# Sums added into the score bank of stick-breaking attention, and the attention layers' low weight halves on VectorE instead of GpSimd

## The chip, the cores and the metric

The kernel is one program on one core of a Trainium2 chip. Its engines are TensorE (PE; PEld is its weight load), VectorE (DVE), ScalarE (ACT), GpSimd (POOL) and SyncE (SP), which issues transfers. The metric is the device time of one execution in microseconds; lower is better.

## What is computed

The reference runs four mixer blocks on a sequence of 512 tokens of width 1024 (pooling, gated convolution, latent attention, pooling again), and behind them two layers that matter here. Each of these computes

```
h    = rmsnorm(x, attn_norm[l])
proj = h @ w_in[l]                      # sb_q, sb_k, sb_v, df_q, df_k, df_v
sb   = stick_breaking_attention(sb_q, sb_k, sb_v)       # 8 heads of 64
df   = differential_attention(df_q, df_k, df_v, lam)    # 4 heads
x    = x + concat(sb, rmsnorm(df) * c) @ w_o[l]
x    = x + square(relu(rmsnorm(x) @ w_ff1[l])) @ w_ff2[l]
```

For a head of the stick-breaking attention, with z the scaled scores of a query against all keys,

```
log_beta = log_sigmoid(z)
log_keep = where(key < query, log_sigmoid(-z), 0)
between  = reversed_cumsum(log_keep) - log_keep          # sum over later keys
w        = where(key < query, exp(log_beta + between), 0)
out      = w @ v
```

With s = softplus(z) = max(z, 0) + log(1 + exp(-|z|)), log_keep is -s and log_beta is z - s, and also min(z, 0) - log(1 + exp(-|z|)).

## The kernel before, in words

Each product of single precision is made of three matmuls on two-part operands: high times high, low times high, high times low (`mm3`, lines 489 to 492; `mm3_on`, lines 494 to 497). A tile of weights ("unit") of 128 rows and up to 1024 columns is loaded into one of four `raw` buffers; ScalarE writes its high part to one of three `wh` buffers (line 1283), and the low part, raw minus high, is written to one of three `wl` buffers by VectorE (line 2109) or by GpSimd in pieces of 256 columns (line 3170). TensorE then waits for `("wlo", n)` and uses the tile in 24 matmuls of 512 columns.

`unit_table` (line 139) lists the units in the order of their use. Its `low(True)` and `low(False)` mark from which unit on the low parts are GpSimd's; a mark takes effect `LOOK` = 2 units later. In each of the two last layers `low(True)` stands ahead of all 32 attention units and `low(False)` ahead of the last, ("wo", 1, 3).

Nothing is scheduled at run time. Each engine has a program of its own, written out by hand as a list of steps, and waits on semaphores for results of the others. In `second_layer(l)` of each engine the list says where it deals with a weight unit (`taking(...)` makes the high or low parts up to two units ahead), a projection (`project`, `turned`, `plain`, `rot`), a head of the stick-breaking attention and a head of the differential attention (`df_...`). VectorE's program had no `taking` in the attention part of these layers, as GpSimd had it.

One head h of the stick-breaking attention goes as follows. Its scores are triangular and are held as three groups of key blocks, (2, 3), (1) and (0), with 384, 384 and 512 columns, each in one of three PSUM banks kept for this purpose (`GR`, `sb_banks`).

- TensorE, `sb_scores(h)` and `sb_cover(h)`: z into bank "ss", with a large negative number added where key >= query.
- ScalarE, `soft(h)`: |z| from the bank (line 1741), exp (line 1745), log (line 1751), into the buffer SA.
- VectorE, `soft(h)`: min(z, 0) - SA into SL (line 2743), then max(z, 0) + SA into SA (line 2746), after which the bank is free.
- ScalarE and VectorE, `keep(h)`: high and low part of SA, SBH and SBL (lines 1292 and 2117).
- TensorE, `sb_between(h)`: sums over later keys, with a triangular matrix of ones `trir` (lines 985 and 986) and a full one `onesr` (lines 990 and 991), into bank "sb", which is the same bank as "ss" in its next use.
- VectorE, `between(h)`: SL minus the sums, into SA (line 2757); the bank is free after it.
- ScalarE, `weights_of(h)`: exp of SA (line 1764) and high part; VectorE: low part.
- TensorE, `sb_pv(h)`: times v (lines 1003 and 1004).

TensorE's order around the steps that are spoken of below, as written in its list:

```
sb_between(3)  df_pv(1)  df_scores(2, 32)  sb_scores(4)  df_scores(2, 16)  sb_cover(4)  proj("dk", 3) ...
df_squares(1)  sb_between(4)  df_turn(2)  proj("sk", 3)  df_pv(2)  df_scores(3, 34)  sb_scores(5) ...
sb_pv(4)  wo(0, 2)  wo(0, 0)  df_scores(3, 16)  sb_between(5)  wo(0, 1)  df_squares(2)  sb_scores(6) ...
sb_between(7)  wo(1, 0, ..)  wo(1, 1, ..)  wo(1, 4, ..)  sb_pv(7)
```

ScalarE's list has `df_turn(1)`, `df_exp(2, 34)`, `df_copy(1)`, `weights_of(3)`; later `df_exp(3, 16)`, `weights_of(5)`. The exponentials of `df_exp` (line 1534) wait for VectorE's `df_max` (lines 2461, 2465, 2468).

Of the kernel before, what the change touches and what calls it, by code (L numbers as in the profile page):

```python
# [138 lines left out]
def unit_table(D):  # L139
# [71 lines left out]
    for l in range(2):  # L211
        qk, v, wo = D[f"qk{l}"], D[f"v{l}"], D[f"wo{l}"]

        low(True)
        for kind, *key in LAYER_UNITS:
            if kind == "v":
                add(("v", l, *key), v[tuple(key)], 1024)
            elif kind == "wo":
                if key == [1, 3]:
                    low(False)  # L220
                add(("wo", l, *key), wo[tuple(key)], 1024)
            else:
                add((kind, l, *key), qk[0, {"sq": 0, "sk": 4, "dq": 8, "dk": 12}[kind] + key[0]], 1024)
# [90 lines left out]
def program(nc, D, out):  # L314
    ctx = ExitStack()
    with ctx:
# [60 lines left out]
        m_before, m_after = OB[:, 0:128], OB[:, 128:256]  # L377
# [29 lines left out]
        SA, SL, SBH, SBL = SETS[0]  # L407
# [59 lines left out]
        def pe_program(handle, c):  # L467
# [399 lines left out]
            def second_layer(l):  # L867
# [112 lines left out]
                def sb_between(h):  # L980
                    for n, (kbs, k0, width) in enumerate(GR):
                        for jb in range(kbs[0], 4):
                            pe.wait_ge(*at("kpl", l, h, {0: 0, 1: 1, 2: 2, 3: 2}[jb]))
                        b = use(sb_banks[n], ("sb", l, h, kbs[0]))
                        pe.do.matmul(b[:, 0:width], trir[:, :], SBH[:, k0:k0 + width], start=True, stop=False)
                        pe.do.matmul(b[:, 0:width], trir[:, :], SBL[:, k0:k0 + width], start=False, stop=False)
                        for jb in range(kbs[0] + 1, 4):
                            o = b[:, 128 * (jb - kbs[0]):512 - 128 * kbs[0]]
                            cc = slice(KOFF[jb], KOFF[jb] + 512 - 128 * jb)
                            pe.do.matmul(o, onesr[:, :], SBH[:, cc], start=False, stop=False)  # L990
                            mm = pe.do.matmul(o, onesr[:, :], SBL[:, cc], start=False, stop=jb == 3)
# [268 lines left out]
        def act_program(handle, c):  # L1260
# [420 lines left out]
            def second_layer(l):  # L1681
# [402 lines left out]
        def dve_program(handle, c):  # L2084
# [92 lines left out]
            def load():  # L2177
# [21 lines left out]
                dve.do.tensor_copy(trir[:, :], m_after)  # L2199
# [458 lines left out]
            def second_layer(l):  # L2658
# [79 lines left out]
                def soft(h):  # L2738
                    for kbs, k0, n in GR:
# [99 lines left out]
                if l == 0:  # L2839
                    scalars()  # L2840
                norms()
                both_norms()
                turn_by_norm()
                v_low(0, 0)
                if l:
                    scalars()
                project("sq", 0)
                plain("sq", 0)
                project("sk", 0)
                plain("sk", 0)  # L2850
                soft(0)
                keep(0)
                turned("dq", 0)
                v_low(0, 1)
                rot("dq", 0)
                between(0)
                turned("dk", 0)
                weights_of(0)
                rot("dk", 0)
# [807 lines left out]
```

## Time and profile before

| | |
|---|---|
| median of 3 runs | 2635.23 us (2634.94 to 2635.53) |
| the profiled execution | 2635.47 us |
| its span, first to last instruction | 2633.7 us |
| granted TensorE clock, mean | 1.000 |
| busy PE / PEld | 2621.3 / 2224.4 us |
| busy DVE / ACT / POOL | 1790.2 / 1310.9 / 608.1 us |

The span is the time from the first to the last instruction of the profiled execution; the execution's own time is 1.8 us longer. Busy times are unions of the instructions' durations. Those of matmuls overlap, because the engine is pipelined and their ends are modelled; the distance of two starts tells more than a duration. The two attention parts lie at about 1457 to 1714 us and 2052 to 2305 us of the span.

### The profile page before, as it was taken

To read this page: it belongs to the slowest core of one execution; us is meant where nothing else is said; L and a number is where in the kernel's file an instruction comes from. 1 tells how busy PE (TensorE), PEld (TensorE's weight loads), DVE (VectorE), ACT (ScalarE), POOL (GpSimd) and SP (SyncE) were. 2 spreads that over 40 slices of the span, in tenths; PEclk is the share of its full clock that TensorE was granted. 3 is DMA by queue.
4 is the path that set the end of the run, shared out by engine and by line. 5 is a ranking of instruction groups with operands and counts; after the bars stand their busy time and mean duration, and the time that the engine had idled before them with its cause. 6 is when DMAs were issued, how large, how long until landed. Compare 5 with 4: busy or idle time off the path is not lost.

```text
span 2633.7 us, 33670 instructions
## 1 busy us (share of the span) xinstructions
PE 2621.3 (100%) x13168; PEld 2224.4 (84%) x13168; DVE 1790.2 (68%) x2771; ACT 1310.9 (50%) x2086; POOL 608.1 (23%) x674
## 2 busy tenths in 40 slices
PE   9999999999999999999999999999999999999999
PEld 7888889899888888888888888888888888888887
DVE  7656576666666646666475768876777568876677
ACT  5323353334346636533225677754445677754445
POOL 0000111011026627510002744420100544420100
PEclk9999999999999999999999999999999999999999
DMA  4233266466322232232222421355651321355650
GB/s 168 96 97 99 89 167 157 132 157 160 111 66 65 69 89 60 73 103 96 96 96 74 124 85 49 110 149 154 176 152 43 106 71 49 122 151 148 176 144 32
DMA packets 92111, 287.13 MB, mean 109 GB/s; under 512 B 10928, under 2 KB 13488, under 8 KB 91952
## 3 DMA queue, kind: packets, MB, share of 16 engines
q1 hardware_dynamic: 80784, 257.18, 30.2%
q0 software_dynamic: 11168, 27.79, 6.4%
q8 instruction: 104, 1.70, 0.3%
q14 instruction: 55, 0.45, 0.1%
HBM read 274.45 MB, written 2.10 MB: 105 GB/s over the span
## 4 chain that ended last, share of the span: by engine, by line
PE 92%; DVE 5%; ACT 2%; issue 0%; POOL 0%; DMA 0%; SPq 0%; DVEq 0%; ACTq 0%
PE ps L490 26%; PE ps L491 26%; PE ps L492 26%; PE ps L497 3%; PE ps L496 3%; PE ps L495 3%; DVE ptl L2117 1%; PE ps L715 1%; PE ps L569 0%; DVE s L2746 0%; DVE s L2743 0%; PE ps L776 0%; PE ps L775 0%; ACT s L1534 0%; ACT s L1745 0%
## 5 line engine op out<-in xcount | busy, mean ns | idle before, releaser
L490 PE MATMUL ps<-xh,wh 128*128 128x512 f32 (+1 forms) x1808 | 696.7, 385 | 0.5 <-POOL wl L3170 0.5
L491 PE MATMUL ps<-xl,wh 128*128 128x512 f32 (+1 forms) x1808 | 692.6, 383 | 0.0
L492 PE MATMUL ps<-xh,wl 128*128 128x512 f32 (+1 forms) x1808 | 692.4, 383 | 0.0
L1283 ACT ACTIVATE wh<-raw 128x1024 fp32r<-128x1024 f32 (+3 forms) x387 | 389.7, 1008 | 481.1 <-PE ps L492 410.7
L2109 DVE TENSOR_TENSOR wl<-raw,wh 128x1024 fp32r<-128x1024 f32 (+2 forms) x277 | 331.2, 1196 | 110.8 <-ACT wh L1283 110.3
L490 PEld LDWEIGHTS ps<-xh,wh 128*128 128x128 f32 x1808 | 340.1, 188 | 67.6 <-POOL wl L3170 1.4
L492 PEld LDWEIGHTS ps<-xh,wl 128*128 128x128 f32 x1808 | 339.9, 188 | 66.6
L491 PEld LDWEIGHTS ps<-xl,wh 128*128 128x128 f32 x1808 | 340.1, 188 | 65.0 <-issue 1.0
L3170 POOL TENSOR_TENSOR wl<-raw,wh 128x256 fp32r<-128x256 f32 x392 | 302.5, 805 | 388.5 <-ACT wh L1283 362.1
L490 PE MATMUL ps<-yh,wh 128*128 128x512 f32 x640 | 251.4, 393 | 0.7 <-ACT s L1534 0.7
L491 PE MATMUL ps<-yl,wh 128*128 128x512 f32 x640 | 249.4, 390 | 0.0
L492 PE MATMUL ps<-yh,wl 128*128 128x512 f32 x640 | 249.4, 390 | 0.0
L3179 POOL TENSOR_TENSOR acc<-acc,t 128x512 f32<-128x512 f32 x44 | 61.7, 1402 | 717.6 <-ACT t L1304 716.3
L1283 ACT ACTIVATE wh<-a 128x1024 fp32r<-128x1024 f32 x96 | 101.9, 1062 | 126.8 <-PE ps L492 64.5
L490 PEld LDWEIGHTS ps<-yh,wh 128*128 128x128 f32 x640 | 120.2, 188 | 27.0 <-POOL wl L3170 2.0
L492 PEld LDWEIGHTS ps<-yh,wl 128*128 128x128 f32 x640 | 120.2, 188 | 25.3
L491 PEld LDWEIGHTS ps<-yl,wh 128*128 128x128 f32 x640 | 120.3, 188 | 23.9
L2109 DVE TENSOR_TENSOR wl<-a,wh 128x1024 fp32r<-128x1024 f32 x96 | 117.1, 1220 | 32.2 <-ACT wh L1283 32.1
L2146 DVE TENSOR_TENSOR x<-ps,x 128x512 f32<-128x512 f32 x96 | 65.4, 687 | 105.6 <-PE ps L492 105.5
L1292 ACT ACTIVATE yh<-t 128x512 fp32r<-128x512 f32 (+1 forms) x148 | 86.1, 584 | 100.4 <-DVE t L2250 56.3
L2117 DVE TENSOR_TENSOR yl<-t,yh 128x512 fp32r<-128x512 f32 (+1 forms) x148 | 99.8, 675 | 36.6 <-ACT yh L1292 36.6
L3103 DVE SCALAR_TENSOR_TENSOR t<-ps,r 128x512 f32<-128x512 f32 x64 | 44.1, 690 | 89.1 <-PE ps L492 88.8
(370 smaller groups left out, 5224.9 us busy)
## 6 DMA issues: line engine op xcount, KB each, us to landing
raw<-in_ff SPq DMA_DIRECT2D x64, 512.0 KB, 5.9
a<-in_ff2t SPq DMA_DIRECT2D x64, 512.0 KB, 7.5
raw<-in_pool_in SPq DMA_DIRECT2D x62, 512.0 KB, 3.4
raw<-in_conv_in SPq DMA_DIRECT2D x50, 512.0 KB, 4.0
raw<-in_pool_out SPq DMA_DIRECT2D x32, 512.0 KB, 3.4
raw<-in_qk SPq DMA_DIRECT2D x32, 512.0 KB, 3.6
sw<-in_conv_in SPq DMA_DIRECT2D x42, 256.0 KB, 3.9
raw<-in_pool_grp SPq DMA_DIRECT2D x16, 512.0 KB, 3.5
```

The source lines that it names most:

```text
L490: pe.do.matmul(o, lh, rh_, start=start, stop=False)
L491: pe.do.matmul(o, lh, rl_, start=False, stop=False)
L492: return pe.do.matmul(o, ll, rh_, start=False, stop=stop)
L495: pe.do.matmul(o, lh, rh_, start=False, stop=False, skip_group_check=True)
L496: pe.do.matmul(o, lh, rl_, start=False, stop=False, skip_group_check=True)
L497: return pe.do.matmul(o, ll, rh_, start=False, stop=stop, skip_group_check=True)
L1283: act.do.activation(h[:, 0:ncol], r[:, 0:ncol], ACT.Copy).then_inc(*mark("whi", ("whi", k)))
L1292: act.do.activation(dst, src, ACT.Copy).then_inc(*mark("act", done))
L2109: dve.do.tensor_tensor(lo[:, 0:ncol], r[:, 0:ncol], f(h[:, 0:ncol]), ALU.subtract).then_inc(*mark("wlo", ("wlo", k)))
L2117: dve.do.tensor_tensor(dst, src, f(h), ALU.subtract).then_inc(*mark("dve", *done))
L2146: dve.do.tensor_tensor(x[m][:, :], ps(*key)[:, :], x[m][:, :], ALU.add).then_inc(*mark("dve", ("psfree",) + key, *done))
L3170: p = pool.do.tensor_tensor(lo[:, cc], r[:, cc], f(h[:, cc]), ALU.subtract)
```

## The change

It does two things in the two last layers.

The sums are added on top of the scores. `sb_between(h)` writes into the bank that still holds z ("ss"), as further matmuls of the same accumulation. The kept values are split with a factor of -1 (ScalarE's copy has scale -1, VectorE's low part is `low_scaled` with -1), so that -s is added, and the triangular matrix is p >= n instead of p > n, so that the sum takes in the key itself: z - s - (sums over later keys). With that SL, line 2743 and the step `between(h)` on VectorE go. ScalarE's `weights_of(h)` takes the exponential from the bank, all three groups first and then the three high parts, and the bank is free after the exponential.

`low(True)` moves from the head of the layer to ("wo", 1, 1). VectorE's list gets a `taking(...)` at each place where the attention units are dealt with.

```
-        low(True)
         for kind, *key in LAYER_UNITS:
...
             elif kind == "wo":
+                if key == [1, 1]:
+                    low(True)
                 if key == [1, 3]:
                     low(False)
...
                 def sb_between(h):
...
-                        b = use(sb_banks[n], ("sb", l, h, kbs[0]))
-                        pe.do.matmul(b[:, 0:width], trir[:, :], SBH[:, k0:k0 + width], start=True, stop=False)
-                        pe.do.matmul(b[:, 0:width], trir[:, :], SBL[:, k0:k0 + width], start=False, stop=False)
+                        b = ps("ss", l, h, kbs[0])
+                        pe.do.matmul(b[:, 0:width], trir[:, :], SBH[:, k0:k0 + width], start=False, stop=False,
+                                     skip_group_check=True)
+                        pe.do.matmul(b[:, 0:width], trir[:, :], SBL[:, k0:k0 + width], start=False, stop=False,
+                                     skip_group_check=True)
...
                     for kbs, k0, n in GR:
-                        high(SBH[:, k0:k0 + n], SA[:, k0:k0 + n], ("kept", l, h, kbs[0]), ("kph", l, h, kbs[0]))
+                        high(SBH[:, k0:k0 + n], SA[:, k0:k0 + n], ("kept", l, h, kbs[0]), ("kph", l, h, kbs[0]), -1.0)
 
                 def weights_of(h):
-                    act.wait_ge(*at("mm", "sb", l, h, 0))
                     for kbs, k0, n in GR:
-                        act.wait_ge(*at("logw", l, h, kbs[0]))
-                        act.do.activation(SA[:, k0:k0 + n], SA[:, k0:k0 + n], ACT.Exp).then_inc(
-                            *mark("act", ("wexp", l, h, kbs[0])))
+                        act.wait_ge(*at("mm", "sb", l, h, kbs[0]))
+                        act.do.activation(SA[:, k0:k0 + n], ps("ss", l, h, kbs[0])[:, 0:n], ACT.Exp).then_inc(
+                            *mark("act", ("wexp", l, h, kbs[0]), ("psfree", "ss", l, h, kbs[0])))
+                    for kbs, k0, n in GR:
                         high(SBH[:, k0:k0 + n], SA[:, k0:k0 + n], ("wexp", l, h, kbs[0]), ("bph", l, h, kbs[0]))
...
-                dve.do.tensor_copy(trir[:, :], m_after)
+                dve.do.tensor_copy(trir[:, :], m_from)
...
                         dve.wait_ge(*at("soft", l, h, kbs[0]))
-                        dve.do.scalar_tensor_tensor(SL[:, k0:k0 + n], src, 0.0, a, ALU.min, ALU.subtract).then_inc(
-                            *mark("dve"))
-                        dve.wait_ge(*mine())
                         dve.do.scalar_tensor_tensor(a, src, 0.0, a, ALU.max, ALU.add).then_inc(
-                            *mark("dve", ("kept", l, h, kbs[0]), ("psfree", "ss", l, h, kbs[0])))
+                            *mark("dve", ("kept", l, h, kbs[0])))
...
                 def keep(h):
                     for kbs, k0, n in GR:
-                        low(SBL[:, k0:k0 + n], SA[:, k0:k0 + n], SBH[:, k0:k0 + n], ("kph", l, h, kbs[0]),
-                            ("kpl", l, h, kbs[0]))
-
-                def between(h):
-                    for kbs, k0, n in GR:
-                        dve.wait_ge(*at("mm", "sb", l, h, kbs[0]))
-                        dve.do.tensor_tensor(SA[:, k0:k0 + n], SL[:, k0:k0 + n], ps("sb", l, h, kbs[0])[:, 0:n],
-                                             ALU.subtract).then_inc(
-                            *mark("dve", ("logw", l, h, kbs[0]), ("psfree", "sb", l, h, kbs[0])))
+                        low_scaled(SBL[:, k0:k0 + n], SA[:, k0:k0 + n], SBH[:, k0:k0 + n], -1.0,
+                                   ("kph", l, h, kbs[0]), ("kpl", l, h, kbs[0]))
```

VectorE's list of steps, cut to the tail of the layer (the rest has `taking` lines of the same kind):

```
                 rot("dq", 2)
+                taking('sk', l, 2)
                 project("sk", 2)
                 project("sq", 2)
                 df_low(0)
+                taking('sq', l, 2)
                 plain("sk", 2)
                 df_turn(1)
                 df_max(2, 34)
                 plain("sq", 2)
-                between(3)
                 weights_of(3)
                 rot("dq", 3)
+                taking('dk', l, 3)
                 df_max(2, 32)
                 df_max(2, 16)
                 soft(4)
...
                 keep(4)
                 df_join(2)
                 turned("dk", 3)
+                taking('sq', l, 3)
                 project("sq", 3)
-                between(4)
                 df_turn(2)
                 df_norm(1)
                 weights_of(4)
                 rot("dk", 3)
+                taking('sk', l, 3)
                 df_low(1)
...
                 sb_out(4)
+                taking('wo', l, 0, 0)
                 df_max(3, 16)
-                between(5)
                 wo_add(0)
                 df_sums(3)
                 df_join(3)
                 weights_of(5)
+                taking('wo', l, 0, 1)
                 wo_add(1)
                 wo_add(4)
                 df_norm(2)
...
                 df_low(2)
-                between(6)
+                taking('wo', l, 0, 2)
                 df_eps(3)
                 sb_out(5)
                 weights_of(6)
                 wo_add(3)
                 wo_add(5)
                 wo_add(6)
+                taking('wo', l, 0, 3)
                 soft(7)
                 keep(7)
+                taking('wo', l, 1, 0)
                 df_norm(3)
                 df_low(3)
-                between(7)
                 sb_out(6)
                 weights_of(7)
```

## Rows read from the trace of the kernel before

**Rows 1.** The page's first part: busy us, share of the span, instructions.

```profile
PE 2621.3 (100%) x13168; PEld 2224.4 (84%) x13168; DVE 1790.2 (68%) x2771; ACT 1310.9 (50%) x2086; POOL 608.1 (23%) x674
```

**Rows 2.** Stretches: length; PE, PEld, DVE, ACT, POOL busy (count); PEclk, DMA, GB/s.

```profile
1600.00:1692.00 92.00, 90.16 (x491) 75.29 (x490) 81.70 (x182) 70.63 (x152) 28.34 (x35) 1.00 0.22 62
1900.00:2000.00 100.00, 100.00 (x443) 82.82 (x442) 71.85 (x96) 45.03 (x54) 6.58 (x8) 1.00 0.42 122
```

**Rows 3.** Waits of PE, whole span: us in total, times, longest.

```profile
PE ps L1003 <- DVE ptl L2117: 1.8, 2, 0.9
...
PE ps L490 <- ACT s L1534: 0.7, 2, 0.3
...
PE ps L490 <- DVE s L2757: 0.6, 2, 0.3
```

**Rows 4.** PE timeline, layer 0: start us, duration us, instruction, [idle before, releaser].

```profile
1599.68 0.42 PE L985 MATMUL ps<-pth,trir 128*128 128x384 f32 x1
...
1605.00 0.28 PE L490 MATMUL ps<-g 64*128 64x256 f32 x1
...
1620.87 0.70 PE L985 MATMUL ps<-pth,trir 128*128 128x384 f32 x1
...
1638.05 0.47 PE L490 MATMUL ps<-yh,wh 128*128 128x512 f32 x1 [0.34 <-ACT s L1534]
...
1644.39 0.28 PE L1021 MATMUL ps<-yh,yl 64*128 64x256 f32 x1
1644.99 0.44 PE L985 MATMUL ps<-pth,trir 128*128 128x384 f32 x1 [0.33 <-DVE ptl L2117]
...
1651.82 0.38 PE L490 MATMUL ps<-g 64*128 64x256 f32 x1 [0.30 <-DVE s L2757]
...
1688.63 0.40 PE L491 MATMUL ps<-yl,wh 128*128 128x512 f32 x1
1688.86 0.39 PE L492 MATMUL ps<-yh,wl 128*128 128x512 f32 x1
1690.12 0.50 PE L1003 MATMUL ps<-pth,values 128*128 128x512 f32 x1 [0.86 <-DVE ptl L2117]
```

**Rows 5.** VectorE's groups, 1480 to 1692 us: count, busy us, mean ns, idle.

```profile
L2743 DVE SCALAR_TENSOR_TENSOR s<-ps,s 128x384 f32<-128x384 f32 x16 | 8.8, 551 | 15.8 <-ACT s L1751 15.7
L2757 DVE TENSOR_TENSOR s<-s,ps 128x384 f32<-128x384 f32 x16 | 8.3, 545 | 4.4 <-PE ps L991 4.4
...
L2757 DVE TENSOR_TENSOR s<-s,ps 128x512 f32<-128x512 f32 x8 | 5.4, 680 | 2.2 <-PE ps L991 2.2
L2743 DVE SCALAR_TENSOR_TENSOR s<-ps,s 128x512 f32<-128x512 f32 x8 | 5.4, 679 | 0.0
```

**Rows 6.** The page's groups of low weight parts, whole span.

```profile
L2109 DVE TENSOR_TENSOR wl<-raw,wh 128x1024 fp32r<-128x1024 f32 (+2 forms) x277 | 331.2, 1196 | 110.8 <-ACT wh L1283 110.3
...
L3170 POOL TENSOR_TENSOR wl<-raw,wh 128x256 fp32r<-128x256 f32 x392 | 302.5, 805 | 388.5 <-ACT wh L1283 362.1
```

**Rows 7.** VectorE's timeline, layer 0.

```profile
1488.61 8.94 DVE L2117 TENSOR_TENSOR ptl<-s,pth 128x384 fp32r<-128x384 f32 x3
...
1516.09 1.62 DVE L2117 TENSOR_TENSOR ptl<-s,pth 128x384 fp32r<-128x384 f32 x3
...
1599.11 1.22 DVE L2117 TENSOR_TENSOR g<-t,g 128x512 fp32r<-128x512 f32 x1
...
1603.48 0.24 DVE L2468 TENSOR_SCALAR small<-small 128x2 f32<-128x2 f32 x1
...
1630.51 0.68 DVE L2117 TENSOR_TENSOR yl<-t,yh 128x512 fp32r<-128x512 f32 x1
...
1651.14 0.17 DVE L2468 TENSOR_SCALAR small<-small 128x4 f32<-128x4 f32 x1
```

**Rows 8.** ScalarE's timeline, layer 0: first exponentials of heads 3 and 5.

```profile
1605.57 0.53 ACT L1764 ACTIVATE s<-s 128x384 f32<-128x384 f32 x1
...
1652.94 0.53 ACT L1764 ACTIVATE s<-s 128x384 f32<-128x384 f32 x1
```

More of the change, by code:

```diff
@@ L406, in program @@
         STACKS = {1: G[12:15], 2: G[15:18], 7: XH[0:3]}
-        SA, SL, SBH, SBL = SETS[0]
+        SA, _, SBH, SBL = SETS[0]
         def v_block(which, part, tb, is_low):
@@ L989, in sb_between @@
                             cc = slice(KOFF[jb], KOFF[jb] + 512 - 128 * jb)
-                            pe.do.matmul(o, onesr[:, :], SBH[:, cc], start=False, stop=False)
-                            mm = pe.do.matmul(o, onesr[:, :], SBL[:, cc], start=False, stop=jb == 3)
+                            pe.do.matmul(o, onesr[:, :], SBH[:, cc], start=False, stop=False, skip_group_check=True)
+                            mm = pe.do.matmul(o, onesr[:, :], SBL[:, cc], start=False, stop=jb == 3,
+                                              skip_group_check=True)
                         mm.then_inc(*mark("group", ("mm", "sb", l, h, kbs[0])))
@@ L2840, in second_layer @@
                     scalars()
+                taking('v', l, 0, 0, 0)
                 norms()
+                taking('v', l, 0, 0, 1)
                 both_norms()
                 turn_by_norm()
+                taking('sq', l, 0)
                 v_low(0, 0)
@@ L2847, in second_layer @@
                 project("sq", 0)
+                taking('sk', l, 0)
                 plain("sq", 0)
@@ L2850, in second_layer @@
                 plain("sk", 0)
+                taking('v', l, 0, 1, 0)
+                taking('dq', l, 0)
                 soft(0)
                 keep(0)
+                taking('v', l, 0, 1, 1)
                 turned("dq", 0)
                 v_low(0, 1)
+                taking('dk', l, 0)
                 rot("dq", 0)
-                between(0)
                 turned("dk", 0)
                 weights_of(0)
+                taking('sq', l, 1)
                 rot("dk", 0)
+                taking('dk', l, 1)
                 project("sq", 1)
@@ L2866, in second_layer @@
                 turned("dk", 1)
+                taking('sk', l, 1)
                 project("sk", 1)
-                between(1)
+                taking('dk', l, 2)
                 df_max(0, 32)
@@ L2875, in second_layer @@
                 turned("dk", 2)
+                taking('dq', l, 1)
                 rot("dk", 1)
                 turned("dq", 1)
+                taking('v', l, 1, 1, 0)
                 soft(2)
+                taking('v', l, 1, 1, 1)
                 df_turn(0)
@@ L2884, in second_layer @@
                 sb_out(1)
+                taking('v', l, 1, 0, 0)
+                taking('v', l, 1, 0, 1)
                 df_max(1, 34)
-                between(2)
                 v_low(1, 0)
+                taking('dq', l, 2)
                 weights_of(2)
@@ L2894, in second_layer @@
                 df_join(1)
+                taking('dq', l, 3)
                 turned("dq", 2)
@@ L2900, in second_layer @@
                 rot("dq", 2)
+                taking('sk', l, 2)
                 project("sk", 2)
@@ L2903, in second_layer @@
                 df_low(0)
+                taking('sq', l, 2)
                 plain("sk", 2)
@@ L2907, in second_layer @@
                 plain("sq", 2)
-                between(3)
                 weights_of(3)
                 rot("dq", 3)
+                taking('dk', l, 3)
                 df_max(2, 32)
@@ L2918, in second_layer @@
                 turned("dk", 3)
+                taking('sq', l, 3)
                 project("sq", 3)
-                between(4)
                 df_turn(2)
@@ L2924, in second_layer @@
                 rot("dk", 3)
+                taking('sk', l, 3)
                 df_low(1)
@@ L2936, in second_layer @@
                 sb_out(4)
+                taking('wo', l, 0, 0)
                 df_max(3, 16)
-                between(5)
                 wo_add(0)
@@ L2942, in second_layer @@
                 weights_of(5)
+                taking('wo', l, 0, 1)
                 wo_add(1)
@@ L2949, in second_layer @@
                 df_low(2)
-                between(6)
+                taking('wo', l, 0, 2)
                 df_eps(3)
@@ L2956, in second_layer @@
                 wo_add(6)
+                taking('wo', l, 0, 3)
                 soft(7)
                 keep(7)
+                taking('wo', l, 1, 0)
                 df_norm(3)
                 df_low(3)
-                between(7)
                 sb_out(6)
```

6 lines of the change are left out of this document (3 added, 3 removed).

## The prediction

> **What bounds the kernel now.** I read the page's first part, then the waits of TensorE, then busy time by stretch, and last the timeline of each engine through one attention layer. The page shows PE busy for practically the whole span [rows 1]. That alone proves little, since matmul ends are modelled; the stretches say more. In a dense part of the feed-forward stage 100 us hold 443 matmuls, 0.226 us each [rows 2], and the whole program is made of such stretches. So the bound is TensorE's own stream, which the change leaves as it is: the same matmuls, of the same shapes, in the same order. The only time to be had or lost is where TensorE waits. Its waits for other engines come to a few microseconds in 2635, nearly all in the two attention layers [rows 3]; a time ascribed there is idle time alone, and the start behind a wait comes later still.
>
> In layer 0 I looked for starts that come too late [rows 4]. The first matmul of sb_pv(7) (1690.12) starts 1.26 us behind its predecessor (1688.86) where 0.23 is usual: 1.03 lost, of which 0.86 are shown as idle, so that a wait costs 0.17 more than its row shows. wo(0, 2), at 1638.05, then lost 0.34 + 0.17 = 0.51, and sb_scores(6), at 1651.82, 0.30 + 0.17 = 0.47, waiting for line 2757, that is, for between(5). sb_between(5), at 1644.99, starts 0.60 behind a matmul of 256 columns, which takes half of 0.23: 0.48, as 0.33 + 0.17 gives too. The first matmul of sb_between(4) (1620.87) lasts 0.70 where its like at head 3 (1599.68) lasts 0.42: 0.28. Together **2.8 us a layer**; layer 1 repeats layer 0, as each wait of rows 3 was met twice. So 5.6 us, 0.2% of the time, is about all that faster helpers can win.
>
> **The change, part by part.**
>
> VectorE's sums. Per head three L2743 (min, subtract) and three L2757 (between) go. One layer's come to 8.8 + 5.4 + 8.3 + 5.4 = 27.9 us [rows 5]. The third instruction of soft (L2746) stays.
>
> Low halves. Per layer 31 weight tiles were flipped to GpSimd (all but the first two, and the first of the feed-forward); after the change two are. So 29 tiles a layer move, 116 GpSimd instructions of 805 ns on the mean, 93 us a layer off GpSimd; VectorE takes 29 of 1.196 us, **34.7 us a layer** [rows 6]. Net, VectorE gets 6.8 us more work a layer. SyncE's loads into a raw buffer wait for the low half and are released about 2 us earlier; nothing waits for them now, so this is worth nothing. ScalarE issues as before, only the order of six instructions changes.
>
> What VectorE gets back. Instructions of it that read two SBUF operands are long while GpSimd works: three lows of keep(0) take 8.94 us where those of keep(1) take 1.62, and one low of 128x512 takes 1.22 at 1599 us where 0.68 is usual (at 1630.51) [rows 7]. With GpSimd nearly idle these 7.3 and 0.54 us come back. The Trainium skill's page SBUF — State Buffer, section "Who interferes with whom", says that a VectorE instruction with two SBUF inputs contends with a GpSimd instruction that reads SBUF and that the later one blocks fully; the rows agree. The large one hid behind projections, as TensorE reached sb_between(0) without waiting; I count nothing for it. The small one lies in the chain of head 4 and enters below.
>
> Weight tiles as such. A full tile feeds 24 matmuls, 5.4 us at 0.226, so three buffers leave some 10 us from a tile's release to its use. A low half on VectorE needs ScalarE's high half, its own 1.2 and its place in VectorE's queue. I expect no wait on a tile; cost 0.
>
> Chain in the scores' bank. Here the change adds a dependence. Before, the score bank came free when VectorE had done between(h); now it is kept until ScalarE has done the exponential of weights_of(h), and on ScalarE that stands behind other work. TensorE's next user is sb_scores(h + 1). I went through the heads by comparing the ScalarE row of the first exponential (L1764) with the start of the next scores. For heads 1, 2, 5 and 7 the exponential is comfortably early, for head 3 just in time. Two places are late.
>
> - Head 4: its scores start at 1605.00 [rows 4]; ScalarE begins the first exponential of head 3 at 1605.57 and ends it at 1606.10 [rows 8], because it first waits for VectorE's maxima (1603.48, rows 7) and does two exponentials and a copy. That is 1.1 us. VectorE also gets a low half (1.2 us, taking('sq', l, 2)) ahead of these maxima and has 0.54 back from the port: 0.6 later. **1.7 us.**
> - Head 6: its scores start at 1651.82; the first exponential of head 5 runs from 1652.94 to 1653.47 [rows 8], behind df_exp(3, 16), whose maxima end at 1651.31 [rows 7]. 1.65 us. Ahead of them VectorE loses three L2743 (1.8 us) and gets taking('wo', l, 0, 0) (1.2 us), but the chain also starts later. Between -0.6 and +1.0, I take 0.35: **2.0 us.**
>
> Where these stalls go. Every wait of rows 4 behind them is one in which TensorE came too soon. With TensorE 1.7 us later, sb_between(4), wo(0, 2) and sb_between(5) find their data (0.28 + 0.51 + 0.48 back). With 2.0 at head 6, in place of its old 0.47, sb_pv(7) finds its own (1.03), and the chain to it loses an instruction of VectorE while a low half (taking('wo', l, 1, 0)) comes in front of df_norm(3): even. A few waits too small for a row of their own may go too; I allow 0.3 for them.
>
> Sum per layer: 3.7 new, 2.8 and 0.3 gone: **+0.6 us**. Twice is +1.2. The profiled execution took 2635.47 us, its span 2633.7; 0.24 more than the median of 2635.23. 2635.47 + 1.2 - 0.24 = **2636.4 us**. Bounds of the terms: head 4 between 0 (the maxima come so early that the exponential is not late) and 2.3; head 6 between 0 and 2.7; the recovered waits between 1.2 and 3.1. Per layer -3.1 to +3.8.
>
> A second rule bears on it. VectorE is busy 81.7 of 92 us in the tail of the layer, 89%, against 72% in the feed-forward stretch [rows 2]. The Trainium skill, Perfetto Trace Analysis, section "Optimizing Scalar/DVE Operations", says that with a saturated DVE offloading to GPSIMD may make sense; it adds that the shared port may spoil it. The first half speaks against this change and is the second rival; the second half for it, and is the first.
>
> **Rivals.**
>
> 1. *VectorE, undisturbed and rid of 48 sums a layer, runs ahead, and both bank waits stay short.* For it: in the tail only nine low halves come (10.8 us) while four heads lose 3.5 us each, so VectorE's load falls there, and 2 to 10 us of contention per layer go. Against: ScalarE's place for the exponentials is fixed behind df_exp. With new waits of 0 to 1 us a layer it gives 2629.0 to 2634. By the port rule above this is what would happen if these chains were VectorE's alone.
>
> 2. *Low halves stand in front of what ScalarE waits for, in the tail, and the delay is not caught up.* The place is taking('sq', l, 2) before df_max(2, 34), taking('wo', l, 0, 0) before df_max(3, 16) and taking('wo', l, 0, 1) before df_turn(3): each is in order on VectorE, and each can itself wait for ScalarE's high half. Price: 1.2 us of work each, 2 with the wait for the high half. If all three count fully and only half of the old waits are recovered, a layer loses 1.1 + 1.65 + 3 x 1.5 - 1.5 = 5.75, and both 11.5: 2646.7. It decides when TensorE loses over 2.6 us a layer net. Against: VectorE still idles over 1 us at several places there.
>
> 3. *Nothing visible*: stalls and recovered waits cancel, 2634 to 2636; part of my forecast's range.
>
> **How the numbers follow.** 0.2% is 5.3 us; about what a measurement of this kernel can tell from no change. Forecast, with its neighbours from 2634 to 2639.5: 0.62, same. Rival 1: 0.23; since the old waits hold only 5.6 us and a little, only 0.06 of it is below 2630. Rival 2: 0.15, of which 0.12 is above 2640.5. Faster 0.06, same 0.82, slower 0.12. The range leaves about 1 in 10 on either side: 2631 to 2641.
>
> **What would show it.** Right: L2743 and L2757 gone; L2109 at 335 instead of 277; GpSimd's L3170 at 160 of 392, VectorE's busy time up by under 14 us; idle time of TensorE before the first scores matmul of heads 4 and 6, released by ScalarE's exponential; sb_pv(7) and wo(0, 2) without a wait; matmul counts and durations as before. Wrong: TensorE waiting for a tile's low half from VectorE, or for the maxima's exponentials; or no wait before the scores of heads 4 and 6; or an attention layer that is shorter than before by over 2 us.

## The result, and the profile after

| | before | after |
|---|---|---|
| median of 5 runs | 2635.43 us (2634.94 to 2636.63) | 2647.44 us (2645.58 to 2649.84) |
| profiled execution / its span | 2635.47 / 2633.7 us | 2647.41 / 2645.4 us |
| granted TensorE clock, mean | 1.000 | 0.996 |

The ratio is 1.0047 [1.0037, 1.0058]: **12.0 us slower**. Forecast was 2636.4 us, with 2631.0 to 2641.0 as the range and "same" as the likeliest. The measured time lies where rival 2 was priced (2646.7 us), but its working is not what happened, as the rows will show.

The work moved as the change says. The page's first part and two of its groups, for the kernel after (its lines are 1 to 15 higher than before; L2109 is now L2113, L3170 is L3185, L1764 is L1767, L1534 is L1538, L490 is L491):

```profile
PE 2627.2 (99%) x13168; PEld 2231.4 (84%) x13168; DVE 1791.3 (68%) x2733; ACT 1302.5 (49%) x2086; POOL 439.4 (17%) x442
...
L2113 DVE TENSOR_TENSOR wl<-raw,wh 128x1024 fp32r<-128x1024 f32 x335 | 408.4, 1220 | 127.4 <-ACT wh L1287 126.4
...
L3185 POOL TENSOR_TENSOR wl<-raw,wh 128x256 fp32r<-128x256 f32 x160 | 123.5, 805 | 264.7 <-ACT wh L1287 264.7
```

Against [rows 1, 6]: the same 13168 matmuls, 58 low halves more on VectorE, 232 pieces fewer on GpSimd, and VectorE's busy time the same to 1.1 us. What differs is when TensorE starts. Its waits, over the whole span (us in total, times, longest):

```profile
PE ps L491 <- ACT s L1767: 7.8, 4, 2.5
PE ps L491 <- DVE g L2121: 1.7, 1, 1.7
```

The three waits of [rows 3] are gone, and no row names a weight tile made by VectorE. The first row is the wait for the scores' bank that the forecast described: two heads in two layers. The second was not in the forecast: the first scores of layer 0. The same three places on TensorE's timeline (start, duration, instruction, idle before and releaser):

```profile
1481.35 0.35 PE L491 MATMUL ps<-g 64*128 64x256 f32 x1 [1.69 <-DVE g L2121]
...
1608.56 0.35 PE L491 MATMUL ps<-g 64*128 64x256 f32 x1 [1.39 <-ACT s L1767]
...
1658.26 0.38 PE L491 MATMUL ps<-g 64*128 64x256 f32 x1 [2.51 <-ACT s L1767]
...
1662.29 0.73 PE L491 MATMUL ps<-yh,wh 128*128 128x512 f32 x1
1662.82 0.63 PE L492 MATMUL ps<-yl,wh 128*128 128x512 f32 x1
1663.25 0.63 PE L493 MATMUL ps<-yh,wl 128*128 128x512 f32 x1
```

The idle times of both views make 9.5 us, and some of that only replaces old waits. So 12 us need something more, and the last three rows have it: matmuls of 512 columns that start 0.43 us apart where 0.226 is usual [rows 2]. The stretches around head 6 (length; PE, PEld, DVE, ACT, POOL busy with counts; granted clock, DMA share, GB/s):

```profile
1655.00:1658.00 3.00, 0.74 (x2) 0.00 (x0) 1.90 (x10) 1.89 (x9) 0.00 (x0) 1.00 0.83 236
1658.00:1660.00 2.00, 1.75 (x9) 1.75 (x10) 2.00 (x11) 2.00 (x6) 0.00 (x0) 0.71 1.04 252
1660.00:1662.00 2.00, 2.00 (x7) 1.25 (x6) 1.99 (x5) 1.97 (x4) 0.00 (x0) 0.50 0.14 38
1662.00:1664.00 2.00, 2.00 (x7) 1.71 (x7) 1.46 (x2) 0.51 (x1) 0.00 (x0) 0.50 0.00 0
1664.00:1666.00 2.00, 2.00 (x7) 1.53 (x7) 0.36 (x1) 0.00 (x0) 0.00 (x0) 0.58 0.48 131
1666.00:1668.00 2.00, 2.00 (x15) 1.79 (x14) 1.10 (x2) 0.67 (x2) 0.00 (x0) 1.00 0.32 131
```

Note the column of the clock. TensorE idles 2.5 us, works again at 1.00 for some half microsecond, and then the granted clock falls to 0.50 (1.2 of 2.4 GHz) for 6.8 us. From 1662 to 1664 us only 4 matmuls of 512 columns start, where 0.226 us each would give 9 (the counts in the rows take in what reaches over an edge). The column PE reads 2.00 of 2.00 all the while: busy time can't tell a slow engine from a full one. The trace of before has no such stretch until its last 2.3 us. In this one there are three ahead of its end: from 1611.06 us (3.4 us long, behind head 4 of layer 0), from 1658.84 (6.8 us, behind head 6) and from 2252.76 (6.8 us, head 6 of layer 1). The last of them begins 0.3 us before the scores start at 2253.09, that is, while TensorE still stands idle. Behind head 4 of layer 1, whose wait was as long as in layer 0, there is none.

**The sum of after.** TensorE runs the same instructions in both traces, so each start can be subtracted from its like (after minus before, in us, running):

| place (line numbers of before) | layer 0 | layer 1 |
|---|---|---|
| scores of head 0 | 0.11 to 1.83: **+1.7** | none |
| scores of head 4 | 2.02 to 3.56: **+1.54** | 7.78 to 9.33: **+1.55** |
| slow clock behind it | 3.56 to 5.17: **+1.6** | none |
| line 490 at 1625, wo(0, 2), sb_between(5) | 5.17 to 4.21: -0.96 | 9.38 to 8.38: -1.00 |
| scores of head 6 | 4.21 to 6.44: **+2.23** | 8.38 to 10.64: **+2.26** |
| slow clock behind it | 6.44 to 9.57: **+3.1** | 10.64 to 13.57: **+2.9** |
| small waits up to sb_pv(7) | 9.57 to 8.75: -0.82 | 13.57 to 12.82: -0.75 |
| sb_pv(7) | 8.75 to 7.61: -1.14 | 12.82 to 11.65: -1.17 |

Bank waits 7.6, start of layer 0 1.7, slow clock 7.7, recovered 2.9 a layer and so 5.8: 11.2. With two drifts of 0.2 ahead of head 4 and 0.1 at the start of the program, these are the 11.7 by which the spans differ. What the chains made and gave back comes to 3.5; without the clock, this would have been a change of 0.13%.

**Why the bank is late.** ScalarE's timeline of after at heads 3 and 5, with its idle time and what ended it:

```profile
1606.11 0.69 ACT L1538 ACTIVATE s<-ps,small 128x512 f32<-128x512 f32 x1 [3.33 <-DVE small L2472]
...
1607.92 1.36 ACT L1767 ACTIVATE s<-ps 128x384 f32<-128x384 f32 x3
...
1656.11 0.37 ACT L1538 ACTIVATE s<-ps,small 128x128 f32<-128x128 f32 x1 [4.74 <-DVE small L2472]
...
1657.70 1.37 ACT L1767 ACTIVATE s<-ps 128x384 f32<-128x384 f32 x3
```

ScalarE is idle for 3.3 and 4.7 us in front of the exponentials of df_exp, which wait for VectorE's maxima; the exponentials that free TensorE's bank stand behind them in its list. Most of this idle time isn't new: before, ScalarE stood 3.05 and 3.74 us at the same two places. New is that TensorE's bank hangs on what comes behind it. VectorE's timeline shows what stands before the maxima at head 6 (the low half of ('wo', l, 0, 0) first) and, in layer 0, before the scores of head 0:

```profile
1652.69 1.21 DVE L2113 TENSOR_TENSOR wl<-raw,wh 128x1024 fp32r<-128x1024 f32 x1
1653.93 0.89 DVE L2465 TENSOR_TENSOR ps<-ps,const 128x128 f32<-128x128 f32 x4
1654.73 1.14 DVE L2469 TENSOR_REDUCE small<-ps 128x1 f32<-128x128 f32 x4
1655.90 0.17 DVE L2472 TENSOR_SCALAR small<-small 128x4 f32<-128x4 f32 x1
...
1470.82 2.31 DVE L2113 TENSOR_TENSOR wl<-raw,wh 128x1024 fp32r<-128x1024 f32 x1
...
1475.22 1.40 DVE L2113 TENSOR_TENSOR wl<-raw,wh 128x1024 fp32r<-128x1024 f32 x1
1476.54 1.77 DVE L2121 TENSOR_TENSOR g<-t,g 128x512 fp32r<-128x512 f32 x1
1478.24 0.68 DVE L2142 TENSOR_TENSOR t<-ps,r 128x512 f32<-128x512 f32 x1
1479.61 1.63 DVE L2121 TENSOR_TENSOR g<-t,g 128x512 fp32r<-128x512 f32 x1 [0.70 <-ACT g L1296]
```

At the start of the layer two low halves that were GpSimd's stand in VectorE's queue ahead of g, the operand of the scores. They are long besides, 2.31 and 1.40 us where 1.21 is usual. In this stretch GpSimd still scales x:

```profile
1470.23 14.38 POOL L3322 TENSOR_TENSOR x<-x,s 128x512 f32<-128x512 f32 x8
```

That the two engines hold each other up here is the rule of the Trainium skill, SBUF — State Buffer, section "Who interferes with whom", which the forecast used for the opposite purpose, as a gain; the durations agree with it. But for g itself this isn't new. Its low halves take 1.77 and 1.63 us here, where [rows 7] have 0.68, and before they were long already, beside GpSimd:

```profile
1473.31 1.24 DVE L2117 TENSOR_TENSOR g<-t,g 128x512 fp32r<-128x512 f32 x1 [0.70 <-ACT g L1292]
...
1475.85 1.66 DVE L2117 TENSOR_TENSOR g<-t,g 128x512 fp32r<-128x512 f32 x1 [0.70 <-ACT g L1292]
```

The second ended at 1477.51 before, 2.0 us ahead of TensorE's use at 1479.49, and ends at 1481.24 now: 3.7 us later, which is what the two low halves take (2.31 + 1.40). So the 1.75 us are their place in the queue. What they take over the usual 1.21 us each is 1.3 us, and that is an estimate of the most that contention can have in it; no run took GpSimd's work away from this stretch.

### The profile page after: what moved, and what is told of

It reads as the page before. It is cut to its first block, busy times and chain, and to the rows that moved or that the text cites. A ratio compares the mean times of both kernels' runs of the same rounds, so it can differ in the third digit from the quotient of the medians.

```text
span 2645.4 us, 33390 instructions
## 1 busy us (share of the span) xinstructions
PE 2627.2 (99%) x13168; PEld 2231.4 (84%) x13168; DVE 1791.3 (68%) x2733; ACT 1302.5 (49%) x2086; POOL 439.4 (17%) x442
## 4 chain that ended last, share of the span: by engine, by line
PE 92%; DVE 4%; ACT 3%; issue 0%; POOL 0%; DMA 0%; SPq 0%; DVEq 0%; ACTq 0%
PE ps L491 26%; PE ps L492 25%; PE ps L493 25%; PE ps L497 3%; PE ps L498 3%; PE ps L496 3%; PE ps L716 1%; DVE wl L2113 1%; ACT s L1538 0%; PE ps L570 0%; PE ps L777 0%; PE ps L776 0%; PE ps L1008 0%; PE ps L994 0%; DVE xl L2125 0%
## 5 line engine op out<-in xcount | busy, mean ns | idle before, releaser
L491 PE MATMUL ps<-xh,wh 128*128 128x512 f32 (+1 forms) x1808 | 696.7, 385 | 0.5 <-POOL wl L3185 0.5
L2113 DVE TENSOR_TENSOR wl<-raw,wh 128x1024 fp32r<-128x1024 f32 x335 | 408.4, 1220 | 127.4 <-ACT wh L1287 126.4
L491 PEld LDWEIGHTS ps<-xh,wh 128*128 128x128 f32 x1808 | 340.4, 188 | 67.3 <-POOL wl L3185 1.4
L491 PE MATMUL ps<-yh,wh 128*128 128x512 f32 x640 | 252.0, 394 | 0.0
L3185 POOL TENSOR_TENSOR wl<-raw,wh 128x256 fp32r<-128x256 f32 x160 | 123.5, 805 | 264.7 <-ACT wh L1287 264.7
L491 PEld LDWEIGHTS ps<-yh,wh 128*128 128x128 f32 x640 | 120.9, 189 | 25.1 <-POOL wl L3185 0.6
L2113 DVE TENSOR_TENSOR wl<-a,wh 128x1024 fp32r<-128x1024 f32 x96 | 117.1, 1220 | 32.2 <-ACT wh L1287 32.2
```

Of the source, the lines that this page charges most:

```text
L491: pe.do.matmul(o, lh, rh_, start=start, stop=False)
L2113: dve.do.tensor_tensor(lo[:, 0:ncol], r[:, 0:ncol], f(h[:, 0:ncol]), ALU.subtract).then_inc(*mark("wlo", ("wlo", k)))
L3185: p = pool.do.tensor_tensor(lo[:, cc], r[:, cc], f(h[:, cc]), ALU.subtract)
```

## The experiments

Two theories were set against each other: the cost comes from the order of the steps that free the scores' bank, and the fall of the clock makes more of each wait; or it comes from the low halves on VectorE, by their load or their place. The kernel before, run beside them, had medians of 2635.19 us (20 runs, for the first four), 2635.52 us (22 runs, for the next four) and 2635.05 us (9 runs, for the last).

### The sums alone

The kernel after, with GpSimd's low halves back. VectorE's `taking` lines stay and have nothing to do.

```
+        low(True)
         for kind, *key in LAYER_UNITS:
...
-                if key == [1, 1]:
-                    low(True)
```

> The changed kernel with the low weight halves of the attention layers back on GpSimd; the sums are still added on top of the scores. Theory A (the waits before the scores of heads 4 and 6 come from the bank that is held until ScalarE's exponential, which stands behind df_exp; TensorE's clock falls behind them): these waits stay, 1.0 to 1.5 us at head 4 and 1.7 to 2.5 us at head 6 in each layer, the clock falls behind the longer one, and the wait before the first scores of layer 0 (1.75 us) goes: 2641 to 2645 us. Rival B (the low halves on VectorE make its maxima late, and that is what TensorE waits for): no wait over 0.6 us at heads 4 and 6, clock 1.00 all through, 2634 to 2636 us.

Measured: 2637.49 us (2633.59 to 2641.13, 10 runs), ratio 1.0006 [0.9997, 1.0016]. One row replaces the first two of after:

```profile
PE ps L490 <- ACT s L1766: 4.6, 4, 1.2
```

The start of layer 0 has no wait now. Head 4 costs 1.36 (with low halves on VectorE: 1.54), head 6 0.77 (with: 2.23). In layer 0 the clock holds, and TensorE leaves the layer 0.7 us earlier than before. In layer 1 it falls at 2197.07 us for 6.8 and at 2248.27 for 3.4 us, which costs 3.1 and 1.6, and TensorE is 3.1 us late at the end. Equal waits with a fall in one layer and none in the other fit the spread of the ten runs over 7.5 us, where before spreads over 2: the mean granted clock is 1.000 in the fastest (2633.59 us) and 0.996 in the slowest. So the sums alone cost next to nothing, and the moved low halves 10 us of the 12, those for the clock included. The median lies between the two theories. Of theory A it keeps the bank waits, the one at head 4 as long as expected; of rival B it has that the low halves in front of the maxima made two thirds of the wait at head 6. The time is below what theory A expected for that reason, and because the clock held in one layer of the profiled execution.

### The low halves alone

```
-        low(True)
...
+                if key == [1, 1]:
+                    low(True)
...
+                taking('sq', l, 2)
```

The kernel before, with the table's new mark and all 29 of VectorE's new lines; the sums stay in a bank of their own.

> The kernel before with only the low weight halves moved to VectorE, at the places of the change; scores and sums keep separate uses of the bank and between(h) stays. Theory A: the wait before the first scores of layer 0 (1.75 us) is there, heads 4 and 6 lose 1 us or less each as before VectorE's between(h) is only somewhat later, the clock keeps its upper level: 2637 to 2640 us. Rival B: VectorE now has both its sums and the low halves, so the waits at heads 4 and 6 are as long as in the changed kernel or longer and the clock falls: 2645 us or more.

Measured: 2655.04 us (2653.14 to 2656.89, 4 runs), ratio 1.0075 [1.006, 1.009]. TensorE's largest waits:

```profile
PE ps L1004 <- DVE ptl L2118: 4.6, 4, 1.5
PE ps L491 <- DVE s L2758: 2.8, 2, 1.4
PE ps L491 <- DVE t L2720: 2.2, 2, 1.1
PE ps L491 <- DVE g L2118: 1.7, 1, 1.7
```

All four name VectorE, which is busy 178.1 of the 212 us from 1480 to 1692, against 155.1 after and 167.2 before. This is what rival B expected. In after the low halves stand at the same places, VectorE has 23 us less to do, and the first three of these waits are gone, as they are in the next kernel, which has no bank waits that could hide them. So load counts here; but the sums also take VectorE's between out of the chain, and no run parts the two. The clock fell twice as well (at 1658.09 and 2258.83 us). The halves don't add: +19.9 for this one, +2.3 for the sums, +12.0 together. Added to this kernel, the sums, which take 27.9 us a layer off VectorE [rows 5], give 7.6 us back. The Trainium skill's page Perfetto Trace Analysis, section "Optimizing Scalar/DVE Operations", whose first half spoke against the change in the prediction, is borne out: GpSimd's help was worth 9 to 20 us here, shared port and all.

### ScalarE frees the bank first

```
+                weights_of(3)
                 df_exp(2, 34)
                 df_copy(1)
-                weights_of(3)
...
+                weights_of(5)
                 df_exp(3, 16)
-                weights_of(5)
```

The kernel after, with these lines of ScalarE's list moved; nothing else.

> The changed kernel with two places of ScalarE's list swapped: weights_of(3) ahead of df_exp(2, 34), and weights_of(5) ahead of df_exp(3, 16). Nothing is computed otherwise. Theory A: both bank waits go, the clock stays at its upper level in the attention layers, the wait of 1.75 us before the first scores stays: 1.5 + 1.4 + 2.2 + 2.3 us less in layer 0 and about 6 less in layer 1, with up to 1.8 a layer of the old waits coming back: 2635.5 to 2639 us. Rival B: the waits move to the next thing that waits for VectorE, the total stays above 2643 us.

Measured: 2637.08 us (2634.61 to 2638.36, 10 runs), ratio 1.0005 [0.9996, 1.0015]; the profiled execution, 2634.61 us, has a mean clock of 1.000 and no fall. The median lies in the range of theory A. The bank waits are gone, the start of layer 0 is as it was, and a wait hidden until now appears:

```profile
PE ps L1007 <- DVE x L2150: 3.3, 2, 1.7
PE ps L491 <- DVE g L2121: 1.7, 1, 1.7
```

Two moved lines give back 10.4 us, though the waits they remove sum to 7.8. VectorE's work is that of after to the instruction, so the order on ScalarE is what ties TensorE's bank to VectorE's maxima: with the order changed neither wait is there. How long the wait at head 6 is comes from both, as without the low halves it was 0.77 and not 2.23. In this trace three waits of 1.7 us stand with no fall of the clock behind them.

### Filling the wait

```
+                def fill(n):
+                    i = ring[0][0]
+                    pe.wait_ge(*at("psfree", *ring[1][i]))
+                    for _ in range(n):
+                        pe.do.matmul(PS[i][:, :], onesr[:, :], VALUES[:, 0:512], start=True, stop=True)
...
+                fill(7)
                 sb_scores(6)
```

The kernel after, with 7 matmuls a layer in the wait of head 6 whose sums nobody reads.

> The changed kernel with seven extra matmuls of 128x512, whose result is thrown away, ahead of the scores of head 6 in each layer, in the next free bank of the ring; they run inside the wait of 3.1 us. If the fall of the clock comes from TensorE standing idle: the scores start at nearly the same time (within 0.5 us), the clock stays at its upper level behind them, and some 2 us a layer come back: 2642.5 to 2645 us. If the clock falls for another reason, it falls as before and the time is 2647 us or more.

Measured: 2646.13 us (2641.52 to 2647.57, 5 runs), ratio 1.0038 [1.0025, 1.0051]. The scores of head 6 come as late as in after (+2.5 in both layers, where they were +2.2). TensorE's own idle time there is 1.0 us now, in front of the 7 matmuls, where it was 2.5. The stretches behind read otherwise:

```profile
1660.00:1662.00 2.00, 2.00 (x13) 1.50 (x11) 1.46 (x9) 2.00 (x7) 0.00 (x0) 1.00 1.07 231
1662.00:1664.00 2.00, 2.00 (x12) 1.56 (x11) 2.00 (x6) 1.97 (x5) 0.00 (x0) 1.00 0.51 129
```

The clock stays at 1.00 in both layers, and from head 6 to sb_pv(7) nothing more is lost (9.41 to 8.60, where after went from 6.44 up to 9.57 and back to 8.75). The median hardly moves, though: 1.3 us. In the profiled execution the clock fell behind the waits that were not filled, at head 0 (from 1484.2 us) and at head 4 (from 1613.91), and a wait of 1.2 us came up at 797 us, in a part that the edit doesn't touch. As a test of the mechanism it holds, if on two places of one execution: no fall behind either, where all four like waits of 2.5 and 3.0 us without filling (two in after, two in the next run) had one. As a saving it is inconclusive.

### A wait alone

```
+                pe.wait_ge(*at("wexp", l, 5, 1))
                 sb_scores(6)
```

The kernel before, with one wait more a layer for an event that no data asks for.

> The kernel before, with one wait added: TensorE waits for the exponential of group (1) of head 5 ahead of the scores of head 6, in both layers; nothing else is changed, and no data asks for this wait. It holds TensorE about 2.7 us longer than its old wait. If idleness of TensorE alone lowers the clock: behind the wait matmuls of 512 columns start 0.43 us apart for some microseconds, another 2.2 us a layer are lost, less 1.0 of the old wait at sb_pv(7): 2642 to 2644 us. If not: 2638 to 2639.5 us.

Measured: 2647.93 us (2647.41 to 2648.48, 4 runs), ratio 1.0044 [1.0031, 1.0058]. The wait, and the stretches behind it in layer 0:

```profile
PE ps L490 <- ACT s L1765: 6.0, 2, 3.0
PE ps L1003 <- DVE ptl L2118: 1.7, 2, 0.9
```

```profile
1650.00:1655.00 5.00, 2.02 (x10) 1.11 (x10) 4.97 (x20) 3.81 (x13) 0.30 (x1) 1.00 0.66 175
1655.00:1660.00 5.00, 5.00 (x17) 3.77 (x17) 3.00 (x7) 3.00 (x5) 1.86 (x3) 0.55 0.35 91
1660.00:1664.00 4.00, 4.00 (x19) 3.37 (x18) 1.10 (x2) 0.66 (x2) 0.93 (x2) 0.70 0.46 131
1664.00:1668.00 4.00, 4.00 (x21) 3.43 (x20) 2.05 (x5) 4.00 (x11) 0.00 (x0) 1.00 0.00 0
```

Each wait moves TensorE back by 2.7 us, and the clock falls at both: in layer 0 from 1655.55 us, 1.3 behind the end of the wait, for 6.8 us, in layer 1 from 2249.47, 0.9 before its end, for 10.2 us. That adds 3.1 and 4.3: two waits of together 5.4 us cost 12.4 in the median. This is the cleanest measure of that price, with every helper's work as before. It is more than the 2642 to 2644 us expected, as the falls cost more than 2.2 each and the old wait didn't go. And the second row is the wait of [rows 3] ahead of sb_pv(7), as long as ever: a stall of TensorE ahead of head 6 doesn't by itself give the old wait back. The likely reason, which no run tests by itself, is that VectorE's chain starts from those same scores and is late with them. With between(6) and between(7) off VectorE it goes even where TensorE is early, as the fastest kernel below shows.

### Two low halves of VectorE moved

```
-                taking('sk', l, 0)
                 plain("sq", 0)
                 project("sk", 0)
                 plain("sk", 0)
+                taking('sk', l, 0)
```

In the second kernel also:

```
-                taking('wo', l, 0, 1)
                 wo_add(1)
                 wo_add(4)
+                taking('wo', l, 0, 1)
```

Both are made from the kernel with ScalarE's two moved lines.

> The kernel with the two swaps on ScalarE (as before) and, on VectorE's list, the low half of taking('sk', l, 0) made after plain('sk', 0) instead of between project('sq', 0) and plain('sq', 0). Theory: the wait of 1.7 us before the first scores of layer 0 is VectorE's queue, one low half of 1.4 us standing in front of what plain('sk', 0) needs; it shrinks to 0.4 us or less, and the time falls by 1.3 to 1.7 us, and the spread of the runs with it as no clock fall can follow: about 2635 us. Rival: GpSimd's scaling of x holds the shared port and the wait stays 1.2 us or more wherever that low half stands: no difference.

> As the run before it, and taking('wo', l, 0, 1) on VectorE after wo_add(1) and wo_add(4) instead of in front. Theory: sb_pv(5) waits 1.7 us in each layer for the bank that wo_add(1) frees, behind that low half of 1.2 us; the wait shrinks to 0.5 us, 2.4 us less in all: 2632 to 2633.5 us, faster than the kernel before. Rival: the low half is late then for wo(0, 3) or in front of df_norm(2) and df_turn(3): the wait moves, no gain.

Measured: 2633.99 us (2633.5 to 2637.1, 11 runs), ratio 0.9995 [0.9987, 1.0004], and 2632.64 us (2631.38 to 2634.68, 11 runs), ratio 0.9988 [0.9979, 0.9997]. The first halves the wait at head 0 (1.7 to 0.8), between what its theory (0.4 or less) and its rival (1.2 or more) expected, and the clock still falls behind it in the profiled execution, at 1482.22 us; the second takes the wait ahead of sb_pv(5) from 1.7 to 0.5 in each layer. By the medians, the first low half that is moved behind what TensorE waits for gives 3.1 us and the second 1.4; the runs of each kernel overlap with those of the one before it. With four lines moved (two of ScalarE, two of VectorE), the whole change is 2.9 us faster than before.

### The sums with ScalarE's order, low halves left on GpSimd

The first kernel of this section with the two moved lines of the third.

> Sums on top of the scores, low halves of the attention layers on GpSimd as before the change, and the two swaps on ScalarE. Theory A with B together (the sums take 28 us a layer off VectorE and are worth something once the bank is given back in time; the low halves only cost): no wait over 0.5 us in either layer and the clock always up: 2630 to 2632 us, the fastest of all. Rival (the low halves on VectorE give back what the shared port costs): not faster than the kernel with the low halves on VectorE and the same swaps.

Measured: **2628.18 us** (2627.67 to 2629.7, 6 runs), ratio 0.997 [0.9959, 0.9982]. All of TensorE's waits for other engines that are left, the largest at the start of the program:

```profile
PE ps L560 <- DVE xl L2181: 1.4, 1, 1.4
PE ps L490 <- POOL wl L3184: 0.5, 1, 0.5
PE ps L569 <- ACT xh L1343: 0.2, 1, 0.2
PE ps L715 <- POOL s L3265: 0.2, 1, 0.2
```

None lies in an attention layer. Each of these layers is 3.5 us shorter than before, the time is below the 2630 to 2632 us expected, the clock is 1.000, and this kernel beats both, by 7.3 and 19.3 us. The low halves on VectorE cost 8.9 us even with ScalarE's order right (2637.08).

### ScalarE's order without the sums

The same two moved lines in the kernel before.

> The kernel before with only ScalarE's two swaps: weights_of(3) ahead of df_exp(2, 34) and df_copy(1), weights_of(5) ahead of df_exp(3, 16). It tells whether the 7 us that the sums on the scores gain with these swaps belong to the sums or to the swaps alone. Theory A: in the kernel before, weights_of(h) waits for VectorE's between(h), which stands behind df_max and a projection on VectorE; ahead of df_exp it would make ScalarE wait and push the exponentials of df_exp back by up to 1 or 2 us, while no bank comes free earlier, since the bank is released by VectorE. So no gain: 2634 to 2640 us, with the old waits of TensorE (up to 0.9 us for VectorE's low part ahead of sb_pv(7)) still there. Rival B: the swaps are good by themselves, because the high and low parts of the weights come earlier; then it lands near 2631 with the old waits shorter, and the sums' own share of the gain is small.

Measured: 2654.18 us (2650.57 to 2654.87, 5 runs), ratio 1.0072 [1.0058, 1.0086]. TensorE's two largest waits, and ScalarE's timeline at weights_of(3):

```profile
PE ps L1016 <- ACT s L1534: 4.9, 2, 2.4
PE ps L715 <- DVE s L2811: 4.2, 2, 2.1
```

```profile
1604.50 0.53 ACT L1764 ACTIVATE s<-s 128x384 f32<-128x384 f32 x1 [4.18 <-DVE s L2757]
...
1607.64 0.67 ACT L1534 ACTIVATE s<-ps,small 128x512 f32<-128x512 f32 x1
```

The direction is that of theory A and the size isn't: 19 us, not up to 5. In the kernel before, weights_of needs VectorE's between, ScalarE stands 4.2 us for it, and df_exp, which TensorE's df_turn needs, moves back; the clock fell three times behind it. So the 7 us of the fastest kernel belong to the pair. The sums free the exponential from VectorE's between, and only then can it go first.

## Why the prediction was wrong

**Right.** TensorE's stream as the bound; the instruction counts; no wait on a weight tile; the chain in the scores' bank, with its two places, its releaser and nearly its size.

- *What VectorE gets back from the port*: keep(0)'s three low parts take 1.62 us (8.94 before, and 10.80 with the sums alone, where GpSimd has its low halves back), and g's low half in the chain of head 4 0.68 (1.22 before).
- *Head 4, 1.7 us*: 1.54 and 1.55. The maxima came 2.4 us later (1605.90 against 1603.48), TensorE itself 2.0 later by then; what is left is 0.4 where the prediction had 0.6.
- *Head 6, "between -0.6 and +1.0, I take 0.35: 2.0 us"*: 2.23 and 2.26, by the same subtraction 4.76 - 4.21 = 0.55 for the 0.35. The low halves make most of it: the sums alone, without any of them, have 0.77.
- *"2.8 and 0.3 gone"*: 2.9 a layer came back. The 2.8 contained 0.47 for head 6's old wait, which was counted twice, as the 2.0 had been taken from a start (1651.82) that already had it in it. The small waits, allowed 0.3, gave more and made up for it. The reason given for sb_pv(7), a TensorE that comes later, was wrong: the kernel with a wait alone keeps that wait, and the fastest kernel loses it.
- *"Nearly all in the two attention layers"*, of TensorE's waits before: 3.8 of 6.4 us were; the rest lies ahead of 809 us and has no part in the change.
- *"About all that faster helpers can win"*, 5.6 us: too low, as the fastest kernel gains 7.3.

So the layer's own sum, 3.8 new and 2.9 gone, is +0.9 where the prediction had +0.6. Two steps failed beside it.

**No term for the low halves at the start of the layer; "I expect no wait on a tile; cost 0".** No tile was waited for, and the contention of keep(0), put at nothing, did cost nothing. But I looked at sb_between(0) and at the tiles' own due times, and not at what the tiles' low halves push back on VectorE: the operand g of the scores of head 0, which come before sb_between(0). 1.7 us in layer 0, nothing in layer 1.

**No term for the clock: 7.7 of 11.7 us, the largest error.** The prediction had "a wait costs 0.17 more than its row shows". That held in the trace of before, whose waits in these layers stay below 0.9 us and whose clock never fell there; the new ones were forecast at 1.7 and 2.0 us, beyond anything that [rows 3] could price. The runs say 3 to 4 us more for one of 2.5 to 3 us, and 1.6 or nothing for one of 1.4. The forecast with these two terms is 2636.4 + 1.7 + 7.7 = 2645.8 us, and with the layer's +0.9 for +0.6 2646.4, 1 us from the median.

**The rivals.** Rival 2 had the right queue (taking('wo', l, 0, 0) in front of df_max(3, 16)) and the right total for a wrong reason: 5.75 us a layer of waits, where the layers had 0.9 net of waits and the clock the rest. Of rival 1 only this is true, that VectorE is less busy in the tail (71.8 of the 92 us from 1600, 81.7 before): it helped nothing, because ScalarE's order held the bank. The sentence against rival 1 said so.

## What to carry to other kernels

When a bank is freed by another engine than before, look at where that engine's list has the freeing instruction and move it forward together with the change: here the sums alone gain nothing (+2 us, within the noise), the two moved lines alone cost 19 us, and together they save 7. Work moved onto a helper is paid where it stands in front of what the bound engine waits for, even if the helper's total stays equal; put it right behind. And price a new wait of TensorE that is longer than any in the trace twice, once for its length and once for what the clock may do behind it.

## What the runs showed of the hardware

Around single waits of TensorE of 1.1 to 3.0 us the granted clock often fell from 1.00 to 0.50, between 0.9 us before TensorE was at work again and 2.7 us after, and stayed there for 3.4 to 10.2 us. Matmuls of 512 columns then start 0.43 us apart where they start 0.23 apart at 1.00. A fall costs about half its length or a little less: 1.6 us for 3.4, 3.1 for 6.8, 4.3 for 10.2, so as much as the wait ahead of it or more. It isn't certain: at head 4 of layer 0 it fell and in layer 1 it didn't behind the same wait. Counted over all the profiled executions, without the filled places and the first 10 us of the program, seven of the eight waits of 2.1 us or more had a fall, and seven of the 23 between 1.0 and 1.7 us; a wait of 0.8 us was followed by one once. Filled with matmuls, the same delay had no fall behind it in two places, and twice the clock fell while TensorE still stood idle, so it is TensorE's idleness that matters and not its lateness. The Trainium skill's page TensorE: Matmul & The Clock Gate, section "A second HAM failure mode: psum-queue depth-cycling", tells of a kernel that cycles through PSUM banks, where frequent short idle spells between groups of matmuls make the clock swing between its two levels; these traces agree as to the swing, and here a single wait for a PSUM bank, of 1.4 or 2.5 us, could do it.
